# Key stage of a two-layer product-key block in whole slabs, with a shorter and interleaved key search and another spacing of the gathered dot products

## What is computed

```python
q = (x @ wq).reshape(b, s, PEER_HEADS, 2, PEER_QUERY_DIM // 2)
sc = jnp.einsum('bshtd,htkd->bshtk', q, subkeys)          # 8 heads, 2 sides, 128 keys
top_s, top_i = lax.top_k(sc, 16)
cand = top_s[..., 0, :, None] + top_s[..., 1, None, :]    # 16 x 16 sums
best_s, best_c = lax.top_k(cand.reshape(b, s, 8, 256), 16)
i1 = jnp.take_along_axis(top_i[..., 0, :], best_c // 16, axis=-1)
i2 = jnp.take_along_axis(top_i[..., 1, :], best_c % 16, axis=-1)
idx, gate = i1 * 128 + i2, jax.nn.softmax(best_s, axis=-1)
hid = jnp.einsum('td,tkd->tk', xb, u[idx])                # u: 16384 x 2048
out = jnp.einsum('tk,tkd->td', jax.nn.gelu(hid) * gate, v[idx])
```

## Time and profile before

| | before |
|---|---|
| median of 3 runs | 3280.0 us (3279.31 to 3281.93) |
| profiled execution, its own time | 3274.78 us |
| its span | 3273.0 us |
| PE, PEld, DVE, ACT, POOL busy | 98%, 84%, 85%, 61%, 12% |
| memory read, written | 951.26 MB, 15.73 MB |
| granted TensorE clock | 0.996 |

### The profile page before, as it was taken

The page is one execution under the profiler, slowest core; times in us unless marked ns, Lnnn a source line. Parts: engine busy times, 40 slices in busy tenths (PEclk is TensorE's granted clock), DMA queues, the critical chain, the costliest instruction groups (busy, mean ns, idle before and its releaser), DMA issues. The chain is left out here.

```text
span 3273.0 us, 52190 instructions
## 1 busy us (share of the span) xinstructions
PE 3196.3 (98%) x19468; PEld 2762.0 (84%) x19468; DVE 2773.5 (85%) x4026; ACT 1997.0 (61%) x3631; POOL 406.6 (12%) x266
## 2 busy tenths in 40 slices
PE   9999999999999999999999999999999999999998
PEld 8888888889888888888888887888888888888887
DVE  5775669999999888888887756999999988888887
ACT  4444556556898755555555545655688875555555
POOL 0000000011111122222100000001111112222220
PEclk9999999999999999999999999999999999999999
DMA  7553345698999989999984344578899999999995
GB/s 273 183 183 140 116 161 192 257 342 339 379 379 378 373 335 372 362 371 367 365 305 156 117 152 158 197 278 338 335 390 380 373 369 366 368 370 368 363 368 224
DMA packets 169221, 969.07 MB, mean 296 GB/s; under 512 B 18912, under 2 KB 52704, under 8 KB 55648
## 3 DMA queue, kind: packets, MB, share of 16 engines
q1 hardware_dynamic: 132192, 698.61, 56.2%
q0 software_dynamic: 36864, 268.45, 22.3%
HBM read 951.26 MB, written 15.73 MB: 295 GB/s over the span
## 5 line engine op out<-in xcount | busy, mean ns | idle before, releaser
L597 ACT ACTIVATE wh<-raw 128x1024 fp32r<-128x1024 f32 x1264 | 1335.5, 1060 | 833.5 <-PE ps L1043 663.9
L1043 PE MATMUL ps<-xx,wh 128*128 128x384 f32 (+1 forms) x5504 | 1333.7, 358 | 6.8 <-DVE xx L1755 4.0
L1043 PE MATMUL ps<-wh,act 128*128 128x512 f32 x3584 | 1190.6, 390 | 0.4 <-issue 0.2
L1746 DVE TENSOR_TENSOR wl<-raw,wh 128x1024 fp32r<-128x1024 f32 x752 | 905.9, 1221 | 323.8 <-ACT wh L597 322.2
L1043 PEld LDWEIGHTS ps<-xx,wh 128*128 128x128 f32 x5504 | 955.5, 189 | 73.5 <-issue 5.7
L1043 PE MATMUL ps<-wl,act 128*128 128x512 f32 x2304 | 897.6, 390 | 0.0
L1043 PEld LDWEIGHTS ps<-wh,act 128*128 128x128 f32 x3584 | 673.8, 188 | 142.0 <-DVE wl L1746 1.0
L1743 DVE SCALAR_TENSOR_TENSOR halves<-raw,wh 128x1024 f16<-128x1024 f32 x512 | 615.2, 1213 | 63.5 <-ACT wh L597 63.1
L1043 PEld LDWEIGHTS ps<-wl,act 128*128 128x128 f32 x2304 | 433.2, 188 | 89.7
L1043 PE MATMUL ps<-halves 128*128 128x192 f16 x4096 | 428.3, 248 | 22.5 <-DVE halves L1743 20.6
L1043 PEld LDWEIGHTS ps<-halves 128*128 128x128 f16 x4096 | 312.7, 98 | 112.4 <-issue 62.8
(11 more groups left out here) (225 smaller groups left out, 1751.2 us busy)
## 6 DMA issues: line engine op xcount, KB each, us to landing
raw<-in_u SPq DMA_DIRECT2D x256, 1024.0 KB, 7.1
raw<-in_v SPq DMA_DIRECT2D x256, 1024.0 KB, 7.4
raw<-in_w SPq DMA_DIRECT2D x118, 1024.0 KB, 4.8
h_scratch<-hring SPq DMA_DIRECT2D x128, 96.0 KB, 7.3
hring<-h_scratch SPq DMA_DIRECT2D x128, 96.0 KB, 7.1
arena<-in_memT SPq DMA_DIRECT2D x4, 512.0 KB, 7.2
raw<-in_w SPq DMA_DIRECT2D x4, 512.0 KB, 7.8
arena<-in_xT SPq DMA_DIRECT2D x4, 512.0 KB, 8.5
```

The costliest lines, as they stand in the source:

```text
L597: nc.scalar.activation(wh[:, j, :], raw_piece(p), ACT.Copy, scale=W_UP if scaled_up(p) else 1.0)\
L1043: return nc.tensor.matmul(out, lhs, rhs, start=start, stop=stop, **kw)
L1746: v.tensor_tensor(wl[:, j, :], raw_piece(p), wh[:, j, :].bitcast(F32), ALU.subtract).then_inc(lo_ready, 1)
```

## The change

Four parts. **Whole slabs:** from the third slab of the key stage on, ACT makes both high pieces in one instruction (`hi_slab`), DVE both rests in one (`low_slab`), and PE does 16 high products and then 16 low ones; the fold of the slab before stands behind the tenth high product. `hi_slab` waits for the high products of the slab two before, `low_slab` for all of that slab. In ACT's list `hi_slab` stands ahead of `take_side`. **Search:** the 256 sums become the 112 that can hold the best 16, two units are taken step by step together, and four units are decoded at once in 16 bits (`batch`). **Dots:** 10 stand in the search (`PAIR_FILL`, `LAST_FILL`), 22 in the rest of the head, one behind every slab's rest from slab 42 to 63, and 32 in the spread trips, one in every second slab. **Positions:** the indices' products stand behind slab 11 and no longer behind slab 19, the transposes of the selection behind slab 47 and no longer behind 63; `compare` is one instruction for both sides.

```diff
-REP_TRIP = 5
+REP_TRIP, SEL_TRIP = 3, 12
+FOLD_AT = 9
-DOT_PIECE = (2, 5, 8, 10, 13, 15)
+COMPARE_SLAB = tuple((p - 1) // 2 for p in Q_PIECE)
+PAIR_FILL = ([("L", "", "L", "", "L", "", "L", "")] * 3
+             + [("S", "S", "", "S", "S", "", "S", "S"), ("S", "S", "S", "S", "S", "", "S", "S"),
+                ("S", "S", "D", "S", "S", "SD", "S", "S"), ("S", "S", "SD", "S", "S", "SD", "S", "S"),
+                ("S", "S", "D", "S", "S", "SD", "S", "S")])
+LAST_FILL = ("S", "D", "S", "D", "S", "D", "S", "D", "S")
+EXP_SLAB, SETUP_SLAB, REST_DOTS = 42, 51, 22
+DOT_SLABS = (1, 3, 5, 7)
+        def hi_slab(p):
+            act.wait_ge(piece_used, p - (RING - 1))
+            act.wait_ge(lo_ready, p - 2)
+            n, j = p // 2, p % RING
+            act.wait_ge(raw_full[n % RAW_SLABS], 16 * (n // RAW_SLABS + 1))
+            nc.scalar.activation(wh[:, j:j + 2, :], raw[:, n % RAW_SLABS, :]
...
-                    ahead = [2 * s + 2, 2 * s + 3]
+                    hi_slab(u0 + 2 * (i * slabs + s + 1))
                     take_side(u0, i * slabs + (s - 1), (s - 1) % 2, ND)
-                    for n in ahead[:-1]:
-                        hi(i * (2 * slabs) + (u0 + n), n % RING)
...
                     gelu(i * slabs + (s - 1), s - 1)
-                    for n in ahead[-1:]:
-                        hi(i * (2 * slabs) + (u0 + n), n % RING)
...
+            pe.wait_ge(hi_ready, piece + 2)
+            for kc in range(KC):
+                last = mm(both, part(wh, kc), xx[:, kc, :, NS:], kc == 0, False, skip_group_check=True)
+                if kc == FOLD_AT and side_of is not None:
                     fold(side_of, 1 - par_, side_t0)
...
+            pe.wait_ge(lo_ready, piece + 2)
+            for kc in range(KC):
...
+                last = mm(side, part(wl16, kc), x16[:, kc // XS, kc % XS, :], False, kc == KC - 1, skip_group_check=True)
...
+            def low_slab():
+                n = next(at_slab)
+                p = u0 + 2 * n
+                j = p % RING
+                dve.wait_ge(hi_ready, p + 2)
+                dve.wait_ge(piece_used, p - 2)
...
+                elif step == 3:
+                    own.mark(v.tensor_tensor(sums[:, 0:4 * TOPK].rearrange("p (a b) -> p a b", a=4),
...
+                    own.mark(v.tensor_tensor(sums[:, 4 * TOPK:].rearrange("p (a b) -> p a b", b=4),
...
+            for n in range(EXP_SLAB + 4, KEPT):
...
+                fill("SD")
```

More of the change, by code:

```diff
@@ L44 @@
 CQ = KC // QX
+XS = 5
 MEM_HEADS, MEM_D = 4, 128
@@ L835, in experts @@
                                  scale=GATE_UP).then_inc(selt_evac, 1)
+            for i in range(SEL_TRIP, HEAD_TRIPS):
+                trip(i, BODY)
             act.wait_ge(gate_split, 2 * (layer + 1))
@@ L1416, in trip @@
                     slab_u(i * (2 * slabs) + (u0 + 2 * s), i * slabs + (t0 + s), s % 2, s, then=then,
-                           side_of=i * slabs + (folded(t0) + s - 1), x_from=QX * layer if first and s == 0 else None,
+                           side_of=i * slabs + (folded(t0) + s - 1), x_from=RING * layer if first and s == 0 else None,
                            side_t0=0 if first and s == 0 else NS)
@@ L1449, in experts @@
             replicate(sel[:, 2, 0:P])
+            with pe.Fori(SEL_TRIP, HEAD_TRIPS) as i:
+                trip(i, BODY)
             for i in range(SPREAD0, SPREAD_END):
@@ L1929, in dot, with fill @@
                                        accum_out=hid[:, j:j + 1]).then_inc(slot_free, 1)
-            def unit(i):
-                head, tail = i < UNITS, i > 0
-                fills = UNIT_FILL[i] if head else UNIT_TAIL
-                done = slice((i - 1) * TOPK, i * TOPK)
-                def fill(gap):
-                    for work in fills[gap]:
-                        if work == "L":
-                            low(1)
-                        else:
-                            dot()
-                    own.sync()
-                if head:
+            def fill(work):
+                for one in work:
+                    if one == "L":
+                        low(1)
+                    elif one == "S":
+                        low_slab()
+                    else:
+                        dot()
@@ new lines, in experts @@
+            for p in range(UNITS // 2):
+                tail = itertools.count() if p and p % 2 == 0 else None
+                for n in range(8):
+                    for i in (2 * p, 2 * p + 1):
+                        unit(i, n)
+                        if tail is not None:
+                            step = next(tail)
+                            if step < 9:
+                                batch(p // 2 - 1, step)
+                            elif p == PEER_H // 2 and step == 10:
+                                own.upto(marked["batch"])
+                                v.scalar_tensor_tensor(out=idx_f, in0=sel[:, 0, 0:P], scalar=float(KEYS),
+                                                       in1=sel[:, 1, 0:P], op0=ALU.mult, op1=ALU.add).then_inc(sidx_ready, 1)
+                    fill(PAIR_FILL[p][n])
+                if p == PEER_H // 2:
@@ L2019, in experts @@
                                     ALU.add).then_inc(idx_ready, 1)
-                unit(i)
+            for n in range(9):
+                batch(UNITS // BATCH - 1, n)
+                fill(LAST_FILL[n])
+            gates = sel[:, 2, :].rearrange("p (u k) -> p u k", k=TOPK)
             own.sync()
-            v.tensor_copy(gsm[:, 0, 0:1], iota[:, 0:1]).then_inc(gd_ready, 1)
-            low(1)
-            dot()
+            own.link(v.tensor_copy(gsm[:, 1, :], gates[:, :, 0]))
+            v.tensor_tensor(gates, gates, gsm[:, 1, :].unsqueeze(2).broadcast_to([P, UNITS, TOPK]), ALU.subtract)\
+                .then_inc(gd_ready, 1)
+            fill("SDSD")
             dve.wait_ge(ge_ready, layer + 1)
-            gates = sel[:, 2, :].rearrange("p (u k) -> p u k", k=TOPK)
             own.mark(v.tensor_reduce(gsm[:, 0, :], gates, AX.X, ALU.add))
-            low(1)
+            fill("SD")
             own.sync()
```

263 lines of the change are left out of this document (140 added, 123 removed).

## The result

The changed kernel takes **3373.3 us** (median of four runs, 3369.6 to 3380.9) against 3279.7 of the kernel before in the same session: a ratio of 1.029, 95% interval 1.027 to 1.031, some 94 us slower. I had forecast slower, by 36 us, and a range that ended at 3342. The direction held, the size did not.

The account below looks back on a forecast made before the run. Beside PE it took DVE in the head, ACT at the fold and transfers in the spread trips as bounds. 2 x (3.5 + 14.4) = +36 on 3274.8 gave 3311, median 3316; range 3240 to 3342.

Parts of the forecast that it names:

- the sum of 3311: Whole kernel: +36 us for two layers on the 3274.8 of the profiled execution before.
- Spread trips: Slab 64 to the last fold: ACT's in-order list makes folds late, 41.6 us a trip, +14.4 us a layer.
- Rival 1: Spread trips: ACT's side is in time, trips near 37.3 us, 3247 us in all; chance 0.22.
- Slabs 15 to 41: Head: DVE needs 116 us against PE's 115, so the search costs nothing there.
- PE's wait for `halves`: Sign in the first 41 slabs: PE's wait for DVE's rests stays under 5 us.
- The first batch: Slab 1: the batch delays the fourth rest, PE stands about 3 us (0 if cheap, 5 at 8 us).
- The positions: Positions and the single `compare` lie in DVE's slack of the trips or behind the head's transfers.
- Slabs 42 to 63: End of the head: one dot a slab makes 5.4 us a slab, slab 64 at 815, +3.5 us a layer.
- full transfers: Slabs 42 to 63: two transfers at 391 GB/s take 5.4 us a slab, DMA share 0.97 or more.
- the turn of a slot: Slabs 42 to 63: dot 2.28, 0.35 to the issue, 8.2 to land, 10.8 us; two slots, 5.4 a slab.
- My upper bound: Head: +14 us with a microsecond more for a gather, 5.9 us a slab.
- A slab of PE: Whole slabs on PE: 4.26 us in place of 4.31, one of two ways to the low products saved.

Follow-up runs that it names:

- few dots: The changed kernel with 6 dots in place of 22 in slabs 42 to 63 and six in place of four in a spread trip: 3312.6 us.
- side first: The changed kernel with `take_side` ahead of `hi_slab` in ACT's list of a slab, everything else as it is: 3309.1 us.
- wide gap: The changed kernel with one added DVE maximum over 512 columns behind each of the 18 dots of slabs 46 to 63: 3362.8 us.
- short gap: The changed kernel with one added DVE maximum over 128 columns behind each of the 18 dots of slabs 46 to 63: 3372.1 us.
- three together: The changed kernel with `take_side` ahead of `hi_slab`, the first batch in pair 3, 14 dots in slabs 42 to 63 and five a trip: 3266.1 us.

## Why the prediction was wrong

The profiled execution took 61 us more than the sum of 3311. The folds give the parts for layers 1 and 2: 7.8 and 7.9 us in slabs 1 to 15, 10.2 and 7.6 to slab 42, 11.3 and 11.1 to slab 64, 5.0 and 4.8 in the trips, less 6.4 in the rest.

- **Spread trips: right.** The chain on ACT was read as 5.45 and 5.19 us and came out as 5.2 to 5.5; a trip was to take 41.6 us and takes 41.85. The stretch costs 19.5 and 20.6 us in place of 14.4: 2 us are the quarter of a microsecond a trip, the rest is the first trip (44.65 us), which is late by what comes out of the head: with few dots there it takes 41.55. Rival 1 failed for the reason given against it, and "side first" shows the point from which it would have held.
- **Slabs 15 to 41, the step that failed.** "116 us, against 115 of PE, and DVE may be a slab ahead" was a sum over 27 slabs, and from it came "the search costs nothing there". It holds as a sum (DVE is busy for 115.2 and 113.5 us of the stretch); PE is late all the same, since the cover is one slab, and DVE's work is not even: five rests, four dots and a batch, 25.4 us, fall on five slabs that PE would do in 21.5. PE waits there, and the products behind the wait of 3.3 us run at the lower clock (0.64 granted from 714.4 to 719.1 us). The stretch takes 125.2 and 122.6 us in place of 115. Moving two dots away gives back 5.4. By the prediction's own sign, PE's wait for `halves` in the first 41 slabs was to be under 5 us; it was 10.7.
- **The first batch, mis-sized.** I had 3 us; it cost 6.7, of which 4.0 are the wait and 2.6 the clock. "No wait below reaches more than two us, so I take the clock to stay" contradicted my own 3 us one paragraph on, and the waits that arose reached 4 us. Nor was the clock 1.00 in both stretches of the kernel before: the earlier trace rows shows the trips alone, and in the head it was 0.96 from 600 to 640 us.
- **The positions, put at nothing.** They were to lie in DVE's slack or behind the transfers; the indices cost PE 2.5 us a layer at slab 11.
- **Slabs 42 to 63, the largest part: the slots' turn right, its term too small.** I gave two reasons for 5.4 us a slab. The first, full transfers, was wrong: the share was 0.89, not the 0.97 that I had named as a sign. The second, the turn of a slot, is what DVE waits for, but it is 12.2 us, not 10.8, and a slab 5.83. I took the landing time of 8.2 us, which counts from the issue, from the trips of before, where a gather is issued in 0.94 us, and did not ask what the issue costs behind a whole rest; 9.5 was measured. The wide gap gives back 5 us a layer, six dots in place of 22 give back 27 to 29. My upper bound, 5.9 a slab for a microsecond more a gather, had the size that came.
- **A slab of PE: 4.29, not 4.26.** Of the 0.05 us a slab that were to go, 0.02 went. Where PE itself is the bound, some 41 slabs, that is 1.2 us a layer.
- **Two slips without weight.** A batch has two instructions over 2048 columns, not three; the sum of 5.6 us has two and is right. The floor of 790.8 for slab 64 is 789.9 by its own terms.
- **The range** took in later transfers and a longer trip, but no term for the clock and none for uneven work under a thin cover. Both made the kernel slower, in both layers.

## What to carry to other kernels

When work is moved to a fuller stretch, compare it with its cover slab by slab, not as a sum over the stretch: a cover of one slab hides one slab's excess. In an in-order list, what stands between a result and its taker is the price of every merge: one instruction of 1.8 us in place of two of 0.95 cost 4.6 us a trip by its place alone, and gained 1 us a trip once it was moved. A gather with two slots needs its dots spaced by the slot's turn (11 to 12 us in the mean here, up to 15), and the instruction behind the dot decides how soon the next gather goes out.

## What the runs showed of the hardware

- The issue of a gather by POOL does not end while DVE runs an instruction with two inputs in SBUF that began at least 0.05 us earlier; it ends 0.81 us behind it. It takes 2.75 us behind a rest of 2.28 and 1.68 behind one of 1.22, and 0.94 when the rest begins less than 0.05 us earlier or up to 0.25 us later. A reduction or a maximum, which read one input, did not hold it up. The rows of POOL above hold both cases: at 703.51 it began 0.35 us into the batch's product of two 16-bit inputs (1.22 us) and took 1.68; at 710.20 it began as far into the one-input reduction and took 0.94.
- A cast reads one input too, and did. With the short gap, an issue that began 0.14 us into a cast of 512 columns took 1.07 us and ended 0.81 behind it too. POOL, then DVE:

```profile
767.79 1.07 POOL L1736 DMA_INDIRECT arena<-in_urows,idx  x1 [3.62 <-DVE arena L1963]
```

```profile
767.65 0.41 DVE L2104 CAST halves<-iota 128x512 f16<-128x512 f32 x1
```

- The Trainium skill ("SBUF — State Buffer", Who interferes with whom) describes the pair of ports that VectorE and GpSimd share as an exclusive lock, and says that a VectorE instruction with two inputs in SBUF contends with a GpSimd instruction that reads SBUF. The trace agrees with that, at 1.68 and 2.75 us in place of 0.94, if the issue of an indirect gather is taken as such a reader, which no run here shows by itself.
- The same section tells of a probe in which a product of two tensors did not hold up a transfer, and gives a reason that it marks as inferred, namely that writing descriptors needs another interface. The measured 1.68 us behind such a product speaks against that for indirect gathers, and the measurement decides.
- A wait of PE of 4.0 us was followed by 5 us at a granted clock of 0.50, in which 16 low products took 2.74 us in place of 1.50 and ten high ones 3.35 in place of 1.99. After a wait of 3.3 us the clock was 0.64 over 4.7 us, and in "three together" after one of 2.1 us also. After one of 1.9 us, ahead of slab 64, ten high products took their usual 1.99.
